# A decoder layer in split fp32r on one core: operand buffers at multiples of 64 bytes, and weight ring slots one 64-byte line further apart

## What is computed

```
h = h + 0.5 * SwiGLU_1(norm(h))              w_ffn1_in (2048 x 11264), w_ffn1_out (5632 x 2048)
z = norm(h) @ w_mix_in                       2048 x 5120, groups B, C, H, U, V
h = h + concat(conv(z), gmlp(z)) @ w_mix_out 2048 x 2048
h = h + cross_attention(norm(h), norm(mem))  w_xq, w_xk, w_xv, w_xo, each 2048 x 2048, 4 heads
h = h + 0.5 * SwiGLU_2(norm(h))              as the first
out = norm(h)
```

## Time and profile before

| | |
|---|---|
| median of 3 runs | 2189.96 us (2189.04 to 2190.95) |
| span of the profiled execution, first to last instruction | 2187.2 us |
| profiled execution's own time | not given apart from the three; 2.8 us lie between its span and the median |
| TensorE busy with matmuls | 2167.1 us, 9626 matmuls |
| VectorE, ScalarE busy | 1349.3 us, 991.6 us |
| read from HBM | 409.01 MB, 188 GB/s over the span |
| TensorE's granted clock, mean | 0.999 |

### The profile page before, as it was taken

How to read it: one execution, slowest core, us unless ns; L and a number is a source line. 1 busy time by engine, 2 the same in 40 slices (tenths; PEclk the granted TensorE clock), 3 DMA queues, 4 the chain that set the end, 5 groups by cost and what they waited for, 6 DMA issues and landing times.

```text
span 2187.2 us, 25558 instructions
## 1 busy us (share of the span) xinstructions
PE 2167.1 (99%) x9626; PEld 1778.9 (81%) x9626; DVE 1349.3 (62%) x1549; ACT 991.6 (45%) x1103; POOL 1.8 (0%) x7
## 2 busy tenths in 40 slices
PE   8999999999999999999999999999999999999998
PEld 6888888888888888888888888888888888888886
DVE  5676667666474547865677554576676667664544
ACT  5444454444343444444554444454444444443433
POOL 0000000000000000000000000000000000000000
PEclk9999999999999999999999999999999999999999
DMA  6666666665556565665556445466666666665553
GB/s 227 209 190 197 195 191 188 197 195 189 188 171 204 181 191 181 195 227 175 180 170 207 155 159 169 157 212 197 193 191 193 192 192 190 195 194 187 188 188 135
DMA packets 159217, 412.20 MB, mean 188 GB/s; under 512 B 12588, under 2 KB 13732, under 8 KB 158756
## 3 DMA queue, kind: packets, MB, share of 16 engines
q1 hardware_dynamic: 157728, 410.04, 60.2%
q10 hardware_dynamic: 1412, 1.11, 0.2%
HBM read 409.01 MB, written 2.10 MB: 188 GB/s over the span
## 4 chain that ended last, share of the span: by engine, by line
PE 96%; DVE 2%; ACT 1%; DMA 0%; issue 0%; ACTq 0%; DVEq 0%
PE ps L906 94%; PE ps L935 1%; DVE w_lo L575 1%; PE ps L919 1%; DVE ps L635 1%; DVE convT L748 0%; DVE xT_lo L583 0%; DMA h<-in_x 0%; ACT convT L444 0%; PE ps L1023 0%; ACT xT_hi L329 0%; ACT w_hi L321 0%; DVE stage L738 0%; ACT scratch L555 0%; ACT zT L441 0%
## 5 line engine op out<-in xcount | busy, mean ns | idle before, releaser
L575 DVE TENSOR_TENSOR w_lo<-raw,w_hi 128x1024 fp32r<-128x1024 f32 x768 | 936.1, 1224 | 773.8 <-ACT w_hi L321 768.6
L321 ACT ACTIVATE w_hi<-raw 128x1024 fp32r<-128x1024 f32 x768 | 811.8, 1061 | 1106.0 <-PE ps L906 1087.0
L906 PE MATMUL ps<-w_hi,xT_hi 128*128 128x512 f32 x1856 | 573.8, 390 | 5.3 <-DVE w_lo L575 5.3
L906 PE MATMUL ps<-w_lo,xT_hi 128*128 128x512 f32 x1856 | 572.2, 389 | 0.0
L906 PE MATMUL ps<-w_hi,xT_lo 128*128 128x512 f32 x1856 | 572.0, 389 | 0.0
L906 PEld LDWEIGHTS ps<-w_hi,xT_hi 128*128 128x128 f32 x1856 | 347.8, 188 | 78.9 <-issue 4.1
L906 PEld LDWEIGHTS ps<-w_lo,xT_hi 128*128 128x128 f32 x1856 | 349.0, 188 | 72.7
L906 PEld LDWEIGHTS ps<-w_hi,xT_lo 128*128 128x128 f32 x1856 | 348.7, 188 | 72.8
L906 PE MATMUL ps<-w_hi,hidT_hi 128*128 128x512 f32 x704 | 223.5, 397 | 0.4 <-DVE w_lo L575 0.4
L906 PE MATMUL ps<-w_hi,hidT_lo 128*128 128x512 f32 x704 | 222.7, 395 | 0.0
L906 PE MATMUL ps<-w_lo,hidT_hi 128*128 128x512 f32 x704 | 221.3, 393 | 0.0
(11 more groups left out here) (119 smaller groups left out, 800.7 us busy)
## 6 DMA issues: line engine op xcount, KB each, us to landing
raw<-in_w_ffn_in SPq DMA_DIRECT2D x352, 512.0 KB, 4.1
raw<-in_w_ffn_out SPq DMA_DIRECT2D x176, 512.0 KB, 4.3
raw<-in_w_mix_in SPq DMA_DIRECT2D x80, 512.0 KB, 4.2
raw<-in_w_mix_out SPq DMA_DIRECT2D x32, 512.0 KB, 3.7
raw<-in_w_xq SPq DMA_DIRECT2D x32, 512.0 KB, 3.8
raw<-in_w_xk SPq DMA_DIRECT2D x32, 512.0 KB, 3.9
raw<-in_w_xv SPq DMA_DIRECT2D x32, 512.0 KB, 3.6
raw<-in_w_xo SPq DMA_DIRECT2D x32, 512.0 KB, 3.6
```

The source lines that it names most:

```text
L321: nc.scalar.activation(w_hi[:, k % RING, :], raw[:, k % RAW, :], ACT.Copy).then_inc(hi_ready, 1)
L575: nc.vector.tensor_tensor(w_lo[:, k % RING, :], raw[:, k % RAW, :], w_hi[:, k % RING, :].bitcast(F32), ALU.subtract).then_inc(lo_ready, 1)
L906: ins = nc.tensor.matmul(bank(s, t * GW + b * BLK, BLK), xs[:, k, t * P:(t + 1) * P], ws_[:, k % RING, b * BLK:(b + 1) * BLK], start=(k == ...
```

## The change

No instruction is added, removed or moved on any engine. Only the starts of buffers in a partition change.

- `xT_hi` and the ring `w_hi` now start at a multiple of 512 bytes, `xT_lo` and the ring `w_lo` 256 bytes past one.
- A ring's slots are 4160 bytes apart in place of 4096, so that slot k starts 64 x k bytes further on in a pitch of 512.
- `extra`, and with it `big` and every buffer from there on, is rounded up to a multiple of 64.

```diff
+    LINE = 64
+    PITCH = 512
+
+    def lines(at, row):
+        return at + (row * LINE - at) % PITCH
+
+    def put(name, shape, dt, at=None, row=None):
...
-            at = place["at"]
-            place["at"] = at + (size + 31) // 32 * 32
+            at = (place["at"] + 31) // 32 * 32
+            if row is not None:
+                at = lines(at, row)
+            place["at"] = at + size
         return nc.alloc_sbuf_tensor_at(name, shape, dt, offset=at)

+    def put_ring(name, dt, skew, row):
+        ring = put(name, [P, RING * (GW + skew)], dt, row=row)
+        return [ring[:, i * (GW + skew):i * (GW + skew) + GW] for i in range(RING)]
+
     h = put("h", [P, TOK, D], F32)
-    xT_hi = put("xT_hi", [P, KD, SEQ], F32R)
-    xT_lo = put("xT_lo", [P, KD, SEQ], F32R)
+    xT_hi = put("xT_hi", [P, KD, SEQ], F32R, row=0)
+    xT_lo = put("xT_lo", [P, KD, SEQ], F32R, row=4)
     raw = put("raw", [P, RAW, GW], F32)
-    w_hi = put("w_hi", [P, RING, GW], F32R)
-    w_lo = put("w_lo", [P, RING, GW], F32R)
+    w_hi = put_ring("w_hi", F32R, LINE // 4, 0)
+    w_lo = put_ring("w_lo", F32R, LINE // 4, 4)
...
-    extra = place["at"]
+    extra = (place["at"] + LINE - 1) // LINE * LINE
...
-                    nc.scalar.activation(w_hi[:, k % RING, :], raw[:, k % RAW, :], ACT.Copy).then_inc(hi_ready, 1)
+                    nc.scalar.activation(w_hi[k % RING], raw[:, k % RAW, :], ACT.Copy).then_inc(hi_ready, 1)
...
-                                                       ws_[:, k % RING, b * BLK:(b + 1) * BLK],
+                                                       ws_[k % RING][:, b * BLK:(b + 1) * BLK],
```

More of the change, by code:

```diff
@@ L104, in build @@
     place = {"at": BASE}
-    def put(name, shape, dt, at=None):
+    LINE = 64
[3 more added lines that the diff above has]
+    def put(name, shape, dt, at=None, row=None):
         size = 4
@@ L161, in build @@
     kT_hi, kT_lo = xT_hi, xT_lo
-    assert big + 2 * KF * KB <= nc.sbuf_usable_end
+    assert big + 2 * KF * KB <= nc.sbuf_usable_end, (big + 2 * KF * KB, nc.sbuf_usable_end)
     vectors = [("g_ffn1", g_ffn1[0], KD), ("g_mix", g_mix[0], KD), ("g_xattn", g_xattn[0], KD), ("g_mem", g_mem[0], KD),
@@ L574, in lo_units @@
                     dve.wait_ge(hi_ready, unit0 + (k + 1))
-                    nc.vector.tensor_tensor(w_lo[:, k % RING, :], raw[:, k % RAW, :], w_hi[:, k % RING, :].bitcast(F32),
+                    nc.vector.tensor_tensor(w_lo[k % RING], raw[:, k % RAW, :], w_hi[k % RING].bitcast(F32),
                                             ALU.subtract).then_inc(lo_ready, 1)
```

## The result

The changed kernel takes **2204.41 us** (median of 4 runs, 2204.02 to 2205.94) against 2189.95 us of the kernel before: the ratio is 1.0067, with a 95% interval of 1.0052 to 1.0081. That is slower by 14.5 us. The forecast was 2165.7 us in a range of 2108 to 2191, so both the sign and the range were wrong. In what follows the *difference* is the start of the moving operand (a slot of `w_hi` or `w_lo`) less that of the stationary operand, in bytes modulo 256.

A forecast was written before the change was run, and what follows sets the result against it. The prediction took TensorE's pace over 9216 dense matmuls as the bound. Part 1 gave 24.3 us and the other parts zero, so 2189.96 - 24.3 = 2165.7 us, with a range of 2108 to 2191.

The forecast's parts named there:

- What bounds the kernel: Whole kernel: the pace of 9216 dense matmuls on TensorE sets the end, 226.7 ns with `xT`, 233.3 with the others.
- every nanosecond is worth 9.2 us: Dense matmuls on TensorE: each nanosecond on one of the 9216 is worth 9.2 us of the time.
- the cover: VectorE, ScalarE and loads: they follow TensorE's faster pace of 2.72 us a unit in ffn_out, in place of 2.80.
- part 1: `hidT`, `yT`, `memT` on multiples of 64: 3648 matmuls gain 6.67 ns each, 24.3 us.
- rival C: Dense matmuls: equal lines of the two operands make the better pace, so the change is slower, 2216.9 us; chance 0.12.
- part 2: Ring slots and `xT` on other 64-byte lines: differing starts for 5/6 of the dense matmuls, taken as zero.
- The bound that stood beside it: Part 2's most loss by the nearest row: 7680 dense matmuls at 233.3 ns, 51 us more than at 226.7.
- A: Dense matmuls, the forecast: alignment of the stationary operand alone decides, 2165.7 us; chance 0.52.
- Part 3: Ring slots: the stagger parts the slot TensorE reads from those ScalarE and VectorE write; taken as zero.
- Part 4: Small matmuls: nothing from transposes; 192 attention matmuls between -2.0 and +1.3 us, taken as zero.
- B: Dense matmuls: the stagger helps too, removing part of the 13.3 ns left with `xT`; 2114.5 or 2080 us; chance 0.26.
- D: Dense matmuls: the two paces come from something the change keeps, so nothing moves, about 2190 us; chance 0.10.

The follow-up runs named there:

- r2: Kernel before, with `hidT`, `yT`, `memT` moved to start at the same place modulo 256 bytes as `xT` and the rings, no stagger; 2166.07 us.
- r3: r2 with every buffer 32 bytes further on, so all dense operands start 32 bytes off a multiple of 64; 2165.83 us.
- r1: Kernel before, with only the region of `hidT`, `yT`, `memT` moved to a multiple of 64 bytes; 2175.14 us.
- r6: Changed kernel with the stagger of the ring slots taken back, all other starts as changed; 2174.59 us.
- r12: Kernel before, with ring slots 256 bytes further apart and `hidT`, `yT`, `memT` placed as in r2; 2165.73 us.
- r4: Kernel before, with slots 16 bytes further apart and `hidT`, `memT`, `yT` moved, so slot-tensor pairs step the difference by 16 bytes through 256; 2212.21 us.
- r10: Kernel before, without stagger, with constant differences: `xT` -16 bytes, `hidT` 16, `memT` -48, `yT` 80; 2237.53 us.
- r8: Kernel before, without stagger, with constant differences: `xT` -32 bytes, `hidT` 32, `memT` 128, `yT` 192; 2223.91 us.
- r7: Kernel before, without stagger, with constant differences: `xT` -8 bytes, `hidT` -40, `memT` 24, `yT` 88; 2247.66 us.
- r11: Kernel before, with all operands on one start modulo 256 except `xT_hi` and `xT_lo`, 8 bytes further on; rings on a multiple of 64; 2187.00 us.

## Why the prediction was wrong

**What bounds the kernel** held: TensorE at the 2.4 GHz level, no wait that matters, the time in the pace of the dense matmuls, two kinds of them with 226.7 and 233.3 ns. So did "every nanosecond is worth 9.2 us", and the cover: VectorE, ScalarE and the DMA followed at the fastest pace in r2 (435.20 and 239.40 us), whose 2166.07 us are what part 1 had given as its sum.

**The step that failed first** is in part 1: "What differs is where the stationary operand starts: `xT` on a multiple of 64 bytes, the three others 32 bytes off one." Two things differed, and the text says so itself under rival C: the start of the stationary operand, and its distance from the moving one. r3 has starts 32 bytes off a multiple of 64 without a distance and runs at 226.7 ns; r1 has the alignment with a distance of 64 bytes and runs at 228.9. The 24.3 us were the worth of an equal start, which the change doesn't give: it gave 7.7 on these matmuls.

**The step that failed with the larger price** is in part 2: "I take zero, by the row nearest to it". The row was the attention's, two pieces of 48 matmuls at 119.8 ns with differences of 96 and 0 bytes. They have 256 columns and not 512, half as long a stream beside the same weight load, and they turned out not to follow the dense ones. The scores have 5.75 us at the difference 96 (before) and at 0 (r2), and 5.65 us at 64 (after, r1): they do depend on the difference, but for them the equal start isn't the best place. They were the wrong row to carry 7680 matmuls. The bound that stood beside it, 51 us, held: measured were 24.5 us on `xT`. Had I weighed C by what the trace could not tell apart, instead of by these two pieces, it would have had at least as good a chance as A.

**Rival C** was right in its mechanism and its sign. Its size was off: 26.9 us net, where the paces gave 16.8. It counted with a pitch of 512 bytes and so had 5/6 of the matmuls off. With the pitch of 256 that r6 and r12 show, one slot in four has the difference 0 and 3/4 are off; its own sum then gives 5568 x 3/4 x 6.67 - 3648 x 1/4 x 6.67 = 21.8 us. The rest is that it took 233.3 ns for every difference, and slots at 64 bytes took 230.3 to 230.5, with an effect of the neighbours on top. So `xT` came to 231.1 ns on average in place of 232.2. The sign it "turns" at, 40% of the matmuls slow, is a count for two paces only.

**Part 3** (stagger against the writers' collisions, zero) held as far as the runs go: r12 parts the slots by 256 bytes and neither gains nor loses against r2, and in the changed kernel the units of the difference 0 settle at 226.7 ns, as without a stagger. The ring instructions kept 1224 and 1060 ns. **Part 4** held within 0.3 us: two pieces of scores gained 0.10 us each. **B** found nothing for it: no run has a steady stretch below 226.7 ns. **D** is out by r2, where `hidT` moved by less than 256 bytes and went from 233.3 to 226.7 ns.

The range left C out whole, at 12%. That was the choice that made the error of the range.

Of the Trainium skill: r3 agrees with the rule on 16-byte lines in "SBUF — State Buffer" as far as 32 bytes off a 64-byte multiple cost nothing (226.7 ns). Its rule doesn't cover what did cost, two contiguous operands 64 bytes apart modulo 256 at 228.9 to 233.3 ns. "TensorE: Matmul & The Clock Gate" says in the step on LDWEIGHTS that loading the next weights takes no read bandwidth from the running matmul. By the prediction's reading of it the stationary start couldn't matter. That reading is refuted: the stationary tensors' place alone moved the pace of 1056 matmuls with `hidT` from 233.3 (before) to 226.7 ns (r2). Whether the load takes bandwidth from the stream, no trace here shows.

**What stays open.** Why an unequal start costs; the trace has no record of memory accesses. Why the same difference has more than one steady pace (64: 228.9 ns in ffn_out, k0 and mix_out, 233.3 in xo1; -16: 226.7 in one slot of r4, 236.7 in r10). Why 256 columns behave otherwise than 512. Which of two neighbouring matmuls pays. Whether the pitch is 256 for every pair: multiples of 256 cost nothing where they were tried (r2, r6, r12), and 128 costs (r8), which leaves no smaller power of two.

## What to carry to other kernels

Where full-rate fp32r matmuls of 512 columns run back to back, let the slices of the moving and of the stationary operands all start at the same place modulo 256 bytes, and keep ring slots at multiples of 256; here that was worth 6.7 ns of 233 on every matmul that had been off, and it costs some padding. Measure other shapes by themselves: the scores, with 256 columns, were 2% faster with the starts 64 bytes apart (5.65 us against 5.75). When two sets of instructions have two paces, list everything in which they differ before naming the cause, relations between operands too, and give the alternatives that the trace can't part like chances. A row with another shape is a weak witness for a null.

## What was not expected of the hardware

- The pace of back-to-back fp32r matmuls of 512 columns depends on where the two operands start with respect to each other: 226.7 ns at equal starts modulo 256 bytes (r2, r3, r12), 228.9 to 240 ns at other constant differences. With 256 columns it depends on it too, but otherwise: 5.75 us for 48 at equal starts (r2), 5.65 us at 64 bytes (r1).
- A steady stretch can settle at different paces with the same instructions, operands and differences, and change from one to the other behind an interruption: 229.0 and 233.3 ns within xo0 of r1, and the same in the layout of r6.
- The first matmuls of a unit are slowed by a slot before them that started elsewhere: in r4, 230.4 ns over the whole of slot 0 of `xT`, 226.7 and 226.8 for its last two gaps.
- At one difference, -8 bytes, `xT` has 236.7 ns in r7 and 230.7 in r11, so the place of the pair counts too. Where the pace is 236.7 (r7, r10) the weight loads take 190 to 191 ns in place of 188.
